# A two-layer transformer trunk on one core: norm roots with tokens on partitions, the first shift vector on TensorE, and another order of the attention units

## The reference: what is computed

```python
sh1, sc1, g1, sh2, sc2, g2 = split(silu(cond) @ w_mod[l] + b_mod[l], 6)   # cond: one vector for the sample, one for the prompt
h = rms_norm(x, norm1[l]) * (1 + sc1) + sh1
y = mixer(h)                      # layer 0: gated convolution and attention; layer 1: windowed attention with sinks and pooling
x = x + g1 * y
h = rms_norm(x, norm2[l]) * (1 + sc2) + sh2
f = swiglu(h) if l == 0 else moe_swiglu(h)      # layer 1: eight experts, each token to two
x = x + g2 * f
# rms_norm(x, g) = x * rsqrt(mean(x * x, over the 1024 features) + 1e-6) * g
# attention: softmax(q k^T / 8) v, 8 query heads on 2 key heads of 64; layer 1 adds exp(sink - max) to the denominator
```

## Time and profile before

| | us |
|---|---|
| median of 3 runs (1880.34 to 1886.09) | 1883.13 |
| the profiled execution | 1881.52 |
| its span, first to last instruction | 1879.8 |

### The profile page before, as it was taken

The page is one execution under the profiler, slowest core; times in us unless marked ns, Lnnn a source line. Parts: engine busy times, 40 slices in busy tenths (PEclk is TensorE's granted clock), DMA queues, the critical chain, the costliest instruction groups (busy, mean ns, idle before and its releaser), DMA issues.

```text
span 1879.8 us, 29748 instructions
## 1 busy us (share of the span) xinstructions
PE 1708.3 (91%) x11829; PEld 1584.2 (84%) x11829; DVE 1150.6 (61%) x1488; ACT 639.4 (34%) x769; POOL 260.1 (14%) x263
## 2 busy tenths in 40 slices
PE   0499889879999999998898989869999999999997
PEld 0499845779999999998796659669999999999997
DVE  7986457886466667567664663455565665655653
ACT  2212255233221221122333442434444444444441
POOL 3010101330000000003001123040110110110100
PEclk9999999889999999999898989979999999999998
DMA  9153100223334444443210001355765665665652
GB/s 361 61 174 123 48 1 0 90 90 120 115 123 156 149 143 158 148 141 113 68 61 10 0 1 68 137 181 180 228 206 172 231 212 181 224 205 185 221 196 62
DMA packets 45260, 251.12 MB, mean 134 GB/s; under 512 B 5472, under 2 KB 6128, under 8 KB 23824
## 3 DMA queue, kind: packets, MB, share of 16 engines
q1 hardware_dynamic: 28176, 192.14, 28.5%
q0 software_dynamic: 16448, 57.88, 10.6%
q10 hardware_dynamic: 576, 0.26, 0.0%
HBM read 236.60 MB, written 13.72 MB: 133 GB/s over the span
## 4 chain that ended last, share of the span: by engine, by line
PE 79%; DVE 9%; issue 6%; ACT 3%; POOL 2%; DMA 1%; SPq 0%; ACTq 0%; DVEq 0%; POOLq 0%
PE pp L625 55%; PE popr L625 5%; PE pm L625 5%; PE popr L810 4%; DVE dump L1286 3%; PE pp L764 2%; PE pp L913 1%; DVE tmpA L1319 1%; PE pm L790 1%; PE popr L807 1%; DVE h_lo L1331 1%; DVE spread L1480 1%; PE pm L793 1%; DVE tmpB L1313 1%; PE pm L869 1%
## 5 line engine op out<-in xcount | busy, mean ns | idle before, releaser
L1643 DVE TENSOR_TENSOR w_lo<-raw,w_hi 128x2048 fp32r<-128x2048 f32 x108 | 247.3, 2291 | 180.0 <-ACT w_hi L1194 180.0
L625 PE MATMUL pp<-g_hi,w_hi 128*128 128x192 f32 x1152 | 317.7, 276 | 6.2 <-DVE tmpB L1681 4.1
L625 PE MATMUL pp<-h_hi,w_hi 128*128 128x320 f32 x1152 | 272.3, 318 | 54.3 <-DVE h_lo L1331 42.2
L625 PE MATMUL pp<-g_lo,w_hi 128*128 128x192 f32 x1152 | 317.4, 276 | 0.0
L625 PE MATMUL pp<-g_hi,w_lo 128*128 128x192 f32 x1152 | 317.2, 275 | 0.0
L625 PE MATMUL pp<-h_lo,w_hi 128*128 128x320 f32 x1152 | 266.6, 313 | 0.0
L625 PE MATMUL pp<-h_hi,w_lo 128*128 128x320 f32 x1152 | 266.0, 312 | 0.0
L625 PEld LDWEIGHTS pp<-h_hi,w_hi 128*128 128x128 f32 x1152 | 196.6, 192 | 62.0 <-issue 61.1
L625 PEld LDWEIGHTS pp<-g_hi,w_hi 128*128 128x128 f32 x1152 | 223.4, 194 | 6.5 <-DVE w_lo L1643 4.3
L625 PEld LDWEIGHTS pp<-g_lo,w_hi 128*128 128x128 f32 x1152 | 223.3, 194 | 0.0
L625 PEld LDWEIGHTS pp<-g_hi,w_lo 128*128 128x128 f32 x1152 | 223.3, 194 | 0.0
(11 more groups left out here) (238 smaller groups left out, 3077.2 us busy)
## 6 DMA issues: line engine op xcount, KB each, us to landing
raw<-in_ws SPq DMA_DIRECT2D x164, 1024.0 KB, 4.8
modraw<-in_wmod POOLq DMA_DIRECT2D x80, 512.0 KB, 3.7
mod_first<-in_wmod SPq DMA_DIRECT2D x4, 2048.0 KB, 19.6
out_y<-six SPq DMA_DIRECT2D x7, 512.0 KB, 3.4
xT<-in_xT SPq DMA_DIRECT2D x1, 2560.0 KB, 20.1
token_rows<-tok SPq DMA_DIRECT2D x5, 512.0 KB, 2.6
mixer<-in_mixer SPq DMA_DIRECT2D x1, 1473.0 KB, 25.1
scond<-in_cond SPq DMA_DIRECT2D x1, 1024.0 KB, 5.1
```

What stands on the lines that cost most here:

```text
L625: ins = mm(out[:, at_bank(lo, hi)], x, y[:, lo:hi], start=f, stop=end)
L1643: V.tensor_tensor(w_lo[b][:], raw[b][:], w_hi[b][:].bitcast(F32), ALU.subtract).then_inc(w_lo_done, 1)
```

## The change

It has two parts.

**Norms and start.** The sums of squares are now made with tokens on partitions: the squares are the stationary operand, a single column of ones the moving one, five matmuls for 640 tokens, into five columns of `pm`. Root and reciprocal are taken over these five columns; DVE spreads the reciprocals over 128 columns each and PE transposes them with a matmul against the identity (`rstd_out`) into `popr`, from which the scaling reads them. In norm 0 POOL adds nothing: PE sums each square itself (`first_sums`). The first shift vector is made on PE: the condition comes also with features on partitions (`condT`), the weights as they are (`wsh`), 16 matmuls of 512 columns give a row of 1024 for each condition, ACT copies the two rows out and PE turns them to columns. Loads of SP are cut and reordered, and POOL asks for its first two modulation tiles only after the turned row.

**Attention.** PE makes the scores of tile k + 1 before the values of tile k, over the border of units too; the maximum scores of the next unit begin in step 0 and the turn stands in step 4. ACT makes the first exponential of the next unit and the halves of the q copy of the unit after next around its copy of `po`; `max_row` stands before the last exponential.

```diff
@@ sync
-            for b in range(4):
-                sp.dma_start(mod_first[b // 2][:, 4 * (b % 2):4 * (b % 2) + 4], wmod_d[4 * b:4 * b + 4].rearrange("t p k -> p t k")
-                             ).then_inc(mod_first_in[b], 16)
-                if b == 1:
-                    sp.dma_start(xT[:], xT_d).then_inc(x_in, 16)
-            for c in range(2):
-                sp.dma_start(raw[c][:], ws_d[c].rearrange("p (k n) -> p k n", k=8)).then_inc(slab_in[c], 16)
...
+            load_scale(0)
+            load_shift(0)
+            load_scale(1)
+            load_shift(1)
+            load_scale(2)
+            load_x(0)
+            load_scale(3)
+            load_x(1)
+            load_shift(2)
+            sp.dma_start(raw[0][:], ws_d[0].rearrange("p (k n) -> p k n", k=8)).then_inc(slab_in[0], 16)
+            load_shift(3)
+            load_shift(4)
+            sp.dma_start(raw[1][:], ws_d[1].rearrange("p (k n) -> p k n", k=8)).then_inc(slab_in[1], 16)
@@ gpsimd
-            squares(0, range(KT - 1))
-
-            pool.wait_ge(mod_first_in[3], 16)
+            pool.wait_ge(sh_turned, 1)
@@ tensor
+            def shift(b):
+
+                pe.wait_ge(sh_in[b], 16)
+                at, n = SHIFT_PARTS[b]
+                for kt in range(at, at + n):
+                    for c in range(2):
+                        last = mm(pp[0][0:2, 512 * c:512 * c + 512], condT[:, kt], mod_first[1][:, kt, 512 * c:512 * c + 512],
+                                  start=kt == 0, stop=kt == KT - 1)
+                return last
...
+            def first_norm():
+
+                pe.wait_ge(condT_ready, 1)
+                shift(0)
+                shift(1)
+                first_sums(range(4))
+                first_sums(range(4, KT))
+                shift(2)
+                shift(3)
+                rstd_out(0)
+                shift(4).then_inc(sh_done, 1)
+                pe.wait_ge(sh_row, 1)
+                for d in range(KT):
+                    last = nc.tensor.transpose(pp[1][:, 2 * d:2 * d + 2], modraw[1][0:2, d * P:(d + 1) * P], ident[0:2, 0:2])
+                last.then_inc(sh_turned, 1)
...
-                    for lo, hi in ((0, HALF), (HALF, TOK)):
-                        last = mm(pm[:, at_bank(lo, hi)], ones, src[:, lo:hi], start=not last_tile, stop=bool(last_tile))
+                    if not last_tile:
+                        mm(pm[:, 0:TT], ident, zero[:], start=True, stop=False)
+                    for t in range(TT):
+                        last = mm(pm[:, t:t + 1], src[:, t * P:(t + 1) * P], ones[:, 0:1], start=False, stop=bool(last_tile) and t == TT - 1)
                 last.then_inc(pm_done, 1)
...
                 if n == 3:
...
+                    for t in range(2):
+                        token_major(t)
+                rstd_out(n)
+                if n == 3:
+                    for t in range(2, TT):
+                        token_major(t)
+
+            def rstd_out(n):
+
+                pe.wait_ge(tok_rstd_wide, n + 1)
+                for t in range(TT):
+                    at = slice(t * P, (t + 1) * P)
+                    last = mm(popr[:, at], tB(0)[:, at], ident, start=True, stop=True)
+                last.then_inc(tok_rstd_out, 1)
...
                 def unit(u, nu, i):
+
                     n = len(attn_tiles(l, u))
-                    for k in range(max(n, 5)):
-                        if k < n:
-                            scores(u, k, i)
-                            if k:
-                                values(u, k - 1, i)
-                        if nu is not None and 1 <= k <= 4:
-                            max_scores(nu, k - 1, i)
-                    if nu is not None:
+                    for k in range(n):
+                        if k + 1 < n:
+                            scores(u, k + 1, i)
+                            if nu is not None and k < 4:
+                                max_scores(nu, k, i)
+                            if nu is not None and k == 4:
+                                turn_max(nu, i)
+                        elif n > 1 and nu is not None:
+                            scores(nu, 0, i)
+                        values(u, k, i)
+                    if n == 1 and nu is not None:
+                        for b in range(4):
+                            max_scores(nu, b, i)
                         turn_max(nu, i)
-                    values(u, n - 1, i)
+                        scores(nu, 0, i)
@@ scalar
                 def unit(u, nu, i):
...
+                    def keep_sums():
+                        act.wait_ge(values_done, i * 12 + (key_step(l, u, n - 1) + 1))
+                        act.wait_ge(out_kept, i * 2 + ((UNITS + 2) * l + u + 1))
+                        A(att_out(u), po, ACT.Copy).then_inc(po_free, 1)
+
+                    def next_first():
+                        act.wait_ge(values_done, i * 12 + (key_step(l, nu) - 2))
+                        exps(nu, 0, i)
...
+                    for k in range(1, n):
+                        if k == n - 1:
+                            max_row(nu, i)
                         exps(u, k, i)
-                        if nu is not None and k == 0:
-                            q_hi(nu, i)
-                    if nu is not None:
-                        max_row(nu, i)
...
+                    next_first()
+                    if later is not None:
+                        q_hi(later, i, (0,))
+                    keep_sums()
+                    if later is not None:
+                        q_hi(later, i, (1,))
...
                 q_hi(0, 0)
                 max_row(0, 0)
                 act.wait_ge(rotated, 5 * l + 5)
+                q_hi(1, 0)
+                exps(0, 0, 0)
                 units(act, unit)
@@ vector
-                step(V.reciprocal(tB(0), tB(0)))
+                step(V.reciprocal(tok_rstd[:], tok_root[:]))
+                V.tensor_copy(tB(0).rearrange("p (t n) -> p t n", n=P), tok_rstd[:].unsqueeze(2).to_broadcast([P, TT, P])
+                              ).then_inc(tok_rstd_wide, 1)
...
+                dve.wait_ge(tok_rstd_out, n + 1)
```

113 lines of the change are left out of this document (80 added, 33 removed).

## The result

The changed kernel takes 1894.8 us (median of 5 runs, 1892.8 to 1897.5) against 1884.1 us for the kernel before (5 runs, 1880.3 to 1886.6): ratio 1.0057, 95% interval 1.0041 to 1.0074. It is slower by 10.7 us, where 4 us less was forecast. Medians in this document are of fast runs: one run of exp_first, of 3420 us, was in the slow state and is left out.

A forecast was written before the change was run, and what follows sets the result against it. TensorE carries 79% of the chain that ended last, so edits pay only where it stands still or runs at its lower clock. -16 - 4.3 + 1 + 2 + 13 = -4.3 on 1883.1 gave 1879 us, range 1858 to 1894.

The forecast's parts named there:

- start to first turn: Start and first norm: shift dots and GpSimd slowing leave the path, first scaling at 50.5 us; -16 us (-22 to -3).
- between the attentions, with norms 1 and 2: Norms 1 and 2: small root and reciprocal start scaling 1.8 to 2.6 us earlier, twice; -4.3 us.
- attention, layer 0: Layer 0's attention: the break moves to the wait for q, units of 11.4 us; +2 us (-2 to +6).
- attention, layer 1: Layer 1's attention: waits for probs and q, units of 13.3 us without falls, plus clock falls; +13 us (+6 to +19).
- norm 3 and the rest: Last norm: ACT copies and roots going out stand ahead, earlier scaling helps nobody; +1 us (-1 to +1.3).
- four at 1.6 now contained: Layer 1's attention: old clock falls set against seven new ones at 1.5 us each; +4 us net.
- Rival (b): No clock fall in the new attention or at the start; layer 0 at 0, layer 1 at +8: 1866 us, chance 0.25.
- Rival (c): Clock falls in every unit of both layers, some twice in a row in layer 1; +14, 1893 us, chance 0.17.
- Rival (a): Attention groups follow without a break: layer 0 units 10.0 us, layer 1 10.9; 1842 us, chance 0.15.
- Rival (d): Start stays on the lower clock, chain ending near 64 us: gain 3, 1892 us; chance 0.05, counted with (c).
- the term for the clock: Start: one clock fall costs 4 us in the second half of the sums and 2 in the next shift matmuls.
- the roots going out: Norms 1 and 2: PE's transposes of the reciprocals, taken at 1.28 to 2.08 us.

The follow-up runs named there:

- exp_first: Changed kernel with layer 1's last exponential moved ahead of the next unit's row of maxima and sink exponential on ScalarE: 1888.5 us.
- fill_q: Changed kernel with 10 matmuls that nothing reads in layer 1's longer stall alone, the wait for q: 1870.6 us.
- late_max: Changed kernel, last exponential before row of maxima, q copy behind the second exponential, first maxima scores behind the first values: 1867.7 us.
- fill_exp: Changed kernel with 6 matmuls that nothing reads in layer 1's shorter stall alone, ahead of the last values: 1888.7 us.
- norms_only: Changed kernel with the attention orders of the kernel before in both layers; new norms and start stay: 1866.2 us.
- start_wide: Changed kernel with the first norm's sums in the old form, ones standing and 640 columns moving; norm 0 scales by wrong values: 1882.8 us.
- start_only: Changed kernel with old attention orders and norms 1 to 3 in their old form; only start and norm 0 stay changed: 1866.2 us.
- start_fill: Changed kernel with one unread 256-column float32 matmul behind the sums of each of the first norm's first seven tiles: 1900.3 us.
- both_orders: Changed kernel with layer 1's last exponential ahead of the row of maxima and, in both layers, both q halves copied ahead of the sums: 1884.3 us.
- fill: Changed kernel with unread matmuls in both stalls of layer 1's intervals, 10 in the wait for q, 6 ahead of the last values: 1872.0 us.

## Why the prediction was wrong

The sum said -4.3, the profiled executions +12.6. Two steps failed above all: the price of a fall of the clock in layer 1's attention, put at 1.5 us where it was 2.7, and the base of that sum, which took the old falls off twice. Step by step, forecast and trace:

| step | forecast | trace | miss |
|---|---|---|---|
| start to first turn | -16 | -14.2 | +1.8 |
| between the attentions, with norms 1 and 2 | -4.3 | -2.0 | +2.3 |
| attention, layer 0 | +2 | +1.2 | -0.8 |
| attention, layer 1 | +13 | +25.9 | +12.9 |
| norm 3 and the rest | +1 | +1.7 | +0.7 |

**Layer 1** carries the miss, in three parts. First a slip of the sum. The +3.9 for six intervals set 13.3 us without a fall against before's mean of 12.7, and that mean already holds before's four falls. Then "four at 1.6 now contained" were taken off once more. Seven new falls at 1.5 are +10.5, not +4; the steps as written give 3.9 + 1.8 + 1.5 + 10.5 = 17.7, where I had 11 and, with the allowance, 13: 4.7 us. Second the price of a fall. The interval without one was right: 13.3 forecast, 13.1 on average in fill_q. But the six intervals of after take 94.9 us, so falls cost (94.9 - 6 x 13.1) / 6 = 2.7 us each and not 1.5: PE works at half speed for about 7 us behind most of q's waits, twice as long as in the rows I took the price from the earlier trace rows. That is 7.3 us, less 1.2 for the interval. Third the first interval and the last two, forecast at +4.8 with their fall, took +7.0.

**Rival (b)**, no fall in the new attention and none at the start, was put at 1866 us. fill_q makes its case for layer 1 alone: +7.2 there, where (b) had +8, and 1870.6 us in all with the start's fall still in it. So its term was sound and its condition wasn't met. **Rival (c)**, the slower one, had the right sign and total (1893), in large part for the wrong place. Its second fall in a row in some units of layer 1 is what came: four of the six intervals have a fall of twice the length. But most of its +14 was the clock falling in layer 0, where none of the six intervals from the second to the eighth turn shows one (11.2 to 11.4 us each), although PE waits about 1 us for q in each. **Rival (a)**, groups that follow without a break, fails by the mechanism the forecast gave: the break moved to the wait for q. late_max shows that it needed q out of ACT's chain. **Rival (d)**, the start on the lower clock to its end near 64 us, didn't come: the roots go out in 1.38 us, at the upper clock.

The Trainium skill ("TensorE: Matmul & The Clock Gate", "Why this matters for your kernels") lets the clock come down after a long unbroken idle gap. The runs don't bear that out as the only way: in after and in fill_exp, with stalls of 1.05 us, it comes down; with the same place filled it doesn't. The Trainium skill ("TensorE: Matmul & The Clock Gate", "A second HAM failure mode: psum-queue depth-cycling") describes short idles between groups of matmuls that make the clock swing. Layer 1 agrees with that (0.79 of full speed), and I had not weighed it.

**The start** had its chain right: loads, sums, shift parts 2 and 3, roots, part 4, the row, the transposes, in this order and with nothing else on the path. Only the term for the clock was small. I let it fall once, for 4 + 2 us; it stayed down for all the sums, 17.0 us instead of 8 x 1.15 (15.0 in norms_only, whose start is the same), and the first scaling came at 53.9 instead of 50.5. The other end of the term, 44.5 if the clock never falls, is close to what start_wide shows with the old form of the sums: 45.3. From the first scaling to the first turn the new kernel gains 1.2 us more.

**Norms 1 and 2**: the term that failed is the roots going out. It was taken between 1.28 and 2.08; it took 2.50 in both norms. Both times PE had stood 1.5 us for root, reciprocal and copy just before, but in norm 3, where it had not, it took 2.24, so that the standing is the cause is not shown. In norm 1 the last sums too took 2.27. The broadcast takes 0.82, not 0.53. And the forecast's own terms add up to a scaling at 410.3 to 411.1, 0.2 us later than it wrote. The 2 us less from sums to scaling were +0.1 in norm 1 and -0.9 in norm 2. Norm 3 was forecast at +1: from the last tile's sums to the first h it is now 9.9 us (1200.26 to 1210.14) against 7.6 (1189.81 to 1197.40), +2.3, of which the routing's matmuls, at a higher clock, gave back 1.7 (8.77 us instead of 10.46). start_only shows the three norms together at no more than the runs can tell apart.

**Layer 0** was right: the wait for q is the longest stall (1.04 against 1.4 forecast), intervals of 11.3 (11.4).

## What to carry to other kernels

Price a stall of TensorE by what stands behind it as well: here an interval with stalls of 0.66 and 1.05 us lost 2.7 us more by the clock. Whether the clock or the wait is what one pays can be told in one run, by filling the stall with matmuls that nothing reads; that a filling fails, as in start_fill, doesn't rule the clock out. When a mean of intervals is the base of a sum, ask whether it already contains the disturbance that the next line takes off. And when an engine's chain sets a wait, taking away another wait ahead of it moves part of the time and doesn't save it (in both_orders 0.66 us went and 0.31 came back).

## What the runs showed of the hardware that I had not expected

- Norm 0's sums with one moving column kept TensorE busy and did not keep its clock up: x80 in a row, no pause, ran at 2.13 us for ten, where the same sums with 640 moving columns a tile ran at 1.15 us with 2.55 us of standing ahead of them and 1.04 us among them. Adding one matmul of 256 columns to each ten (start_fill) did not stop the fall; it cost 1 us each. A short run of the one-column form can stand at the upper clock: norm 2's took 1.25 and 1.29 us for ten.
- The place of a stall decides, not only its length. In layer 0 about 1 us in every interval left the clock up, in layer 1 1.05 us brought it down for 3.4 to 7 us. There a shorter stall ends 1.2 us ahead of it, and a matmul of one row (L887) follows it, which layer 0 has not. Filling the longer one was enough (fill_q), filling the shorter was not (fill_exp: 128.9 us). Whether it is the one-row matmuls that make layer 1 sensitive was not tried, so why layer 0 is spared stays open.
- The clock varies from run to run of one kernel: fill's four runs took 1865.2, 1869.4, 1874.6 and 1880.3 us, at a mean granted clock of 0.961, 0.957, 0.952 and 0.954. The slowest is not the one with the lowest clock, so it isn't the clock alone.
